# Attention of a hybrid encoder: one maximum over two banks of scores, and turned tiles copied in pairs

## What is computed

```python
s = jnp.einsum('bkgqd,bskd->bkgqs', qi, k, preferred_element_type=F32) * scale
p = jax.nn.softmax(s, axis=-1).astype(v.dtype)
return jnp.einsum('bkgqs,bskd->bkgqd', p, v)
```

## Time and profile before

| what | value |
|---|---|
| median of three runs | 1513.63 us (1511.82 to 1513.84) |
| the profiled execution's own time | 1511.2 us |
| its span in the profile | 1508.5 us |
| mean granted TensorE clock | 0.957 of full |
| attention of the first layer in the span | about 196 to 314 us |
| attention of the second layer in the span | about 933 to 1051 us |

### The profile page before, as it was taken

The page is one execution under the profiler, slowest core; times in us unless marked ns, Lnnn a source line. Parts: engine busy times, 40 slices in busy tenths (PEclk is TensorE's granted clock), DMA queues, the critical chain, the costliest instruction groups (busy, mean ns, idle before and its releaser), DMA issues.

```text
span 1508.5 us, 14989 instructions
## 1 busy us (share of the span) xinstructions
PE 1386.0 (92%) x5763; PEld 1033.6 (69%) x5763; DVE 912.5 (60%) x981; ACT 597.3 (40%) x931; POOL 518.4 (34%) x239
## 2 busy tenths in 40 slices
PE   5999887888999999999979989787979999999997
PEld 4677654455788888878746766454758888887885
DVE  4766776545687777711176776664467887884212
ACT  4422356533534433422242225564344344333222
POOL 2322311015444444344451222100354444444444
PEclk7999998988999999999989999898989999999997
DMA  7211210002233333323241221000213333332331
GB/s 246 83 36 49 49 30 15 1 29 83 70 89 93 98 97 87 92 88 100 82 139 51 61 49 44 15 1 0 71 56 98 91 91 98 98 89 87 99 94 66
DMA packets 203695, 109.93 MB, mean 73 GB/s; under 512 B 14615, under 2 KB 201865, under 8 KB 202730
## 3 DMA queue, kind: packets, MB, share of 16 engines
q1 hardware_dynamic: 203626, 108.98, 24.7%
HBM read 105.69 MB, written 2.10 MB: 71 GB/s over the span
## 4 chain that ended last, share of the span: by engine, by line
PE 78%; DVE 10%; ACT 6%; issue 2%; POOL 2%; DMA 1%; DVEq 0%; POOLq 0%; SPq 0%; ACTq 0%
PE ps L921 20%; PE ps L923 19%; PE ps L922 19%; PE ps L1212 3%; PE ps L1015 2%; PE ps L1028 2%; PE ps L989 2%; PE ps L1188 2%; ACT prob L722 2%; PE ps L1080 1%; DVE p L1427 1%; POOL xT L451 1%; ACT wh L503 1%; PE ps L931 1%; DVE tb L1339 1%
## 5 line engine op out<-in xcount | busy, mean ns | idle before, releaser
L444 POOL TENSOR_TENSOR wl<-raw,wh 128x1024 fp32r<-128x1024 f32 x184 | 447.3, 2432 | 871.7 <-ACT wh L503 871.7
L503 ACT ACTIVATE wh<-raw 128x1024 fp32r<-128x1024 f32 x184 | 195.0, 1060 | 613.3 <-PE ps L923 595.7
L921 PE MATMUL ps<-gh,wh 128*128 128x512 f32 (+1 forms) x896 | 365.7, 408 | 2.7 <-POOL wl L444 2.7
L922 PE MATMUL ps<-gl,wh 128*128 128x512 f32 (+1 forms) x896 | 355.5, 397 | 0.0
L923 PE MATMUL ps<-gh,wl 128*128 128x512 f32 (+1 forms) x896 | 355.3, 397 | 0.0
L921 PEld LDWEIGHTS ps<-gh,wh 128*128 128x128 f32 (+1 forms) x896 | 168.0, 187 | 49.7 <-issue 8.1
L922 PEld LDWEIGHTS ps<-gl,wh 128*128 128x128 f32 (+1 forms) x896 | 167.9, 187 | 45.8 <-issue 5.1
L923 PEld LDWEIGHTS ps<-gh,wl 128*128 128x128 f32 (+1 forms) x896 | 167.8, 187 | 42.1
L1735 DVE SCALAR_TENSOR_TENSOR cv<-pad,pm,cv 128x512 f32<-128x512 f32 x88 | 130.5, 1483 | 84.1 <-ACT cv L823 84.1
L1323 DVE TENSOR_TENSOR acc<-acc,sq 128x512 f32<-128x512 f32 x24 | 60.5, 2520 | 195.8 <-ACT sq L547 195.6
L921 PE MATMUL ps<-fh,wh 128*128 128x512 f32 x352 | 139.5, 396 | 3.2 <-POOL wl L444 3.2
(11 more groups left out here) (231 smaller groups left out, 1902.4 us busy)
## 6 DMA issues: line engine op xcount, KB each, us to landing
raw<-w_up SPq DMA_DIRECT2D x88, 512.0 KB, 3.8
raw<-w_down SPq DMA_DIRECT2D x32, 512.0 KB, 3.6
raw<-w_in SPq DMA_DIRECT2D x30, 512.0 KB, 3.8
raw<-w_out SPq DMA_DIRECT2D x16, 512.0 KB, 3.6
raw<-w_down SPq DMA_DIRECT2D x16, 384.0 KB, 3.1
xio<-x SPq DMA_DIRECT2D x4, 512.0 KB, 4.2
win<-c_win SPq DMA_DIRECT2D x2, 1024.0 KB, 4.9
TF<-c_tf SPq DMA_DIRECT2D x2, 1024.0 KB, 8.8
```

Source lines behind the costliest of these rows:

```text
L444: nc.gpsimd.tensor_tensor(wl[:, slot, :], raw[:, slot, :], wh[:, slot, :].bitcast(F32), ALU.subtract).then_inc(S["lo_ready"], 1)
L503: A(wh[:, slot, :], raw[:, slot, :], ACT.Copy).then_inc(S["hi_ready"], 1)
L921: mm(ps[0:cols, bank, :], w_hi, x_hi, start=start and k == 0, stop=False)
L922: mm(ps[0:cols, bank, :], w_hi, x_lo, start=False, stop=False)
```

## The change

Three things are changed, all inside the attention of both layers.

1. `maxima` takes one instruction for two banks: it reads `ps[:, 0:2, :]` and writes two columns of `nm`, then the same for banks 2 and 3. It waits for both tiles of scores, and the exponentials of both tiles wait for it.
2. ScalarE's `pt_copy(h)` copies banks 4 and 5 in one instruction after the first half of the turning (key tiles 0 and 1). It stands where the copy of tile 0 stood; the copy of tile 2 is gone from ScalarE.
3. VectorE's `pt_copy(h)` copies banks 4 and 5 in one instruction after the second half (key tiles 2 and 3). It stands where the copy of tile 3 stood; the copy of tile 1 is gone from VectorE. So `turn(h, (2, 3))` waits for ScalarE's copy alone, and `turn(h + 1, (0, 1))` and `inverses` wait for VectorE's.

```diff
--- before.py
+++ after.py
@@ -712,7 +712,7 @@
                         A(yh[:, c0 + c, :], src[:, c, :], ACT.Copy).then_inc(S["ygh"], 1)
 
                 def exp(h, qc):
-                    act.wait_ge(S["nmax"], (lay * HEADS + h) * TC + qc + 1)
+                    act.wait_ge(S["nmax"], (lay * HEADS + h) * 2 + qc // 2 + 1)
                     if h >= 2 and qc == 0:
 
                         act.wait_ge(S["pt_tile"], lay * 4 * HEADS + 4 * (h - 1))
@@ -722,13 +722,13 @@
                     A(prob[:, h % 2, qc, :], ps[:, qc, :], ACT.Exp, bias=nm[:, h % 2, qc:qc + 1], scale=1.0,
                       accum_out=den[:, (h // 2) % 2, h % 2, qc:qc + 1]).then_inc(S["p_ready"], 1)
 
-                def pt_copy(h, sc):
-
-                    act.wait_ge(S["pt_tile"], lay * 4 * HEADS + 4 * h + sc + 1)
-                    if h >= 3 and sc == 0:
+                def pt_copy(h):
+
+                    act.wait_ge(S["pt_tile"], lay * 4 * HEADS + 4 * h + 2)
+                    if h >= 3:
 
                         act.wait_ge(S["pv"], lay * PAIRS + (h - 1) // 2)
-                    A(probT[h % 3][:, sc, :], ps[:, 4, :], ACT.Copy).then_inc(S["pt_act"], 1)
+                    A(probT[h % 3][:, 0:2, :], ps[:, 4:6, :], ACT.Copy).then_inc(S["pt_act"], 1)
 
                 def inv_wide(p):
 
@@ -754,13 +754,12 @@
                     if more:
                         exp(h + 1, 0)
                         exp(h + 1, 1)
-                    pt_copy(h, 0)
+                    pt_copy(h)
                     if more:
                         exp(h + 1, 2)
                         exp(h + 1, 3)
                     if h + 2 < GH:
                         q_hi(h + 2)
-                    pt_copy(h, 2)
                     if h and h % 2 == 0:
                         inv_copy(h // 2 - 1)
                     if h % 2:
@@ -1177,10 +1176,12 @@
                     if h == 0:
                         pe.wait_ge(S["evac"], lay * WIN + WIN)
                     for sc in tiles_:
-                        if sc >= 2 or h:
-
-                            k = (lay * HEADS + h) * 2 + sc // 2
-                            pe.wait_ge(S["pt_act" if sc % 2 == 0 else "pt_dve"], k)
+                        if sc % 2 == 0:
+
+                            if sc:
+                                pe.wait_ge(S["pt_act"], lay * HEADS + h + 1)
+                            elif h:
+                                pe.wait_ge(S["pt_dve"], lay * HEADS + h)
                         if sc == 0 and h % 2 and h >= 3:
 
                             pe.wait_ge(S["inv_copy"], lay * PAIRS + h // 2)
@@ -1203,8 +1204,8 @@
                         pe.wait_ge(S["y_pair"], lay * PAIRS + p)
                     if p == GH // 2:
                         pe.wait_ge(S["b7_free"], lay * len(B7) + len(B7))
-                    pe.wait_ge(S["pt_act"], (lay * HEADS + 2 * p + 1) * 2 + 2)
-                    pe.wait_ge(S["pt_dve"], (lay * HEADS + 2 * p + 1) * 2 + 2)
+                    pe.wait_ge(S["pt_act"], lay * HEADS + 2 * p + 2)
+                    pe.wait_ge(S["pt_dve"], lay * HEADS + 2 * p + 2)
                     for sc in range(TC):
                         for half in range(2):
                             h = 2 * p + half
@@ -1223,7 +1224,7 @@
                         bank7(B7_FIRST[h])
                     turn(h, (2, 3))
                     if h and h % 2 == 0:
-                        pe.wait_ge(S["pt_act"], (lay * HEADS + h) * 2 + 2)
+                        pe.wait_ge(S["pt_dve"], lay * HEADS + h + 1)
                         inverses(h // 2 - 1)
                     if h == 0:
                         bank7(B7_FIRST[0])
@@ -1234,7 +1235,7 @@
                     if h == 9:
                         group(1)
                 values(PAIRS - 1)
-                pe.wait_ge(S["pt_act"], (lay * HEADS + HEADS) * 2)
+                pe.wait_ge(S["pt_dve"], lay * HEADS + HEADS)
                 inverses(PAIRS - 1)
 
 
@@ -1498,9 +1499,10 @@
                     tt(dst[:], src[:], hi_[:].bitcast(F32), ALU.subtract).then_inc(S["mlo"], 1)
 
                 def maxima(h):
-                    for qc in range(TC):
-                        dve.wait_ge(S["s_tile"], (lay * HEADS + h) * 4 + qc + 1)
-                        nc.vector.reduce_max(nm[:, h % 2, qc:qc + 1], ps[:, qc, :], AX.X, negate=True).then_inc(S["nmax"], 1)
+                    for qc in range(0, TC, 2):
+                        dve.wait_ge(S["s_tile"], (lay * HEADS + h) * 4 + qc + 2)
+                        nc.vector.reduce_max(nm[:, h % 2, qc:qc + 2], ps[:, qc:qc + 2, :], AX.X, negate=True
+                                             ).then_inc(S["nmax"], 1)
 
                 everything = slice(0, P)
 
@@ -1601,13 +1603,13 @@
                         dve.wait_ge(S["ygh"], lay * DC + c0 + c + 1)
                         tt(yl[:, c0 + c, :], src[:, c, :], yh[:, c0 + c, :].bitcast(F32), ALU.subtract).then_inc(S["ygl"], 1)
 
-                def pt_copy(h, sc):
-
-                    dve.wait_ge(S["pt_tile"], (lay * HEADS + h) * 4 + sc + 1)
-                    if h >= 3 and sc == 1:
+                def pt_copy(h):
+
+                    dve.wait_ge(S["pt_tile"], (lay * HEADS + h) * 4 + 4)
+                    if h >= 3:
 
                         dve.wait_ge(S["pv"], lay * PAIRS + (h - 1) // 2)
-                    copy(probT[h % 3][:, sc, :], ps[:, 5, :]).then_inc(S["pt_dve"], 1)
+                    copy(probT[h % 3][:, 2:4, :], ps[:, 4:6, :]).then_inc(S["pt_dve"], 1)
 
                 def rotate_kr():
 
@@ -1660,12 +1662,11 @@
                 for h in range(HEADS):
                     if h + 1 < HEADS:
                         maxima(h + 1)
-                    pt_copy(h, 1)
                     if h % 2:
                         denominators(h // 2)
                     if h in B7_FIRST and h:
                         bank7(B7_FIRST[h])
-                    pt_copy(h, 3)
+                    pt_copy(h)
                     if h == 0:
                         bank7(B7_FIRST[0])
                     if h and h % 2 == 0:
```

## The result

The changed kernel takes 1532.33 us in the median (1531.0, 1531.43 and 1533.23 us), against 1513.36 us in four executions of the kernel before: ratio 1.013, 95% interval 1.0106 to 1.0154. It is slower by 19 us. A fourth execution of the changed kernel took 2348 us with a granted clock of 0.58 over its whole length, and is not compared.

A forecast was written before the change was run, and what follows sets the result against it. No engine is full; attention is a ring of waits. Lost overlap of 8.3 us per layer, 16.5 for both, plus 2.2 for the clock makes 18.7 on 1513.6: 1532 us, range 1521 to 1543.

The forecast's parts named there:

- faster rival: Attention, 24 heads: VectorE's busy time sets the pace and gains 0.20 us per head, 4.8 us: 1509; chance 0.04.
- (a): Before the exponentials: the first one waits for a maximum of 1.22 us instead of 0.68, +0.54 us.
- (b): In front of the turning's second half: ScalarE's copy takes 1.02 us instead of 0.60, +0.42 us.
- (c): Behind the turning's second half: VectorE's copy waits for both tiles, inverses start after 2.40 us, not 1.35: +1.05 us.
- the gates: Attention places where an engine waits for a piece made longer, by (a), (b) or (c); 16.5 us in both layers.
- The sum over the heads: Attention, heads 0 to 11: costs of waits less head 11's gain, 8.3 us per layer, 16.5 us for both.
- the cover: Head 1: a gap where VectorE idles 1.03 us takes in the later second half; cost 0, without it 0.9.
- Head 11: Last head: second half waits for ScalarE alone, turned during VectorE's four gains, one copy follows: -1.2 us per layer.
- One more stretch per layer: Attention: longer idling drops TensorE to the lower clock once more per layer, at 1.1 us, +2.2 us in both.
- The clock rival: Attention: most lengthened gaps slow TensorE's clock, five more stretches per layer, +11 to +16 us, about 1543; chance 0.16.
- Half the terms hidden: Attention: other waits stand behind the gates, the five (c) terms fall away; costs 8 us, about 1522; chance 0.17.
- No change: Attention: gains at the last head and on VectorE balance the gates, 1514; chance 0.05.

The follow-up runs named there:

- e3: Kernel before, with only ScalarE's copy of the first half of the turning made wide: 1516.4 us, ratio 1.0026.
- e7: Kernel before, with wide maxima and wide first copies of ScalarE only at heads where the forecast has them hidden: 1512.6 us, ratio 1.0003.
- e8: Kernel before, with wide maxima and wide first copies of ScalarE only at heads where the forecast has them waited for: 1520.4 us, ratio 1.005.
- e9: Changed kernel, with unread matmuls laid into TensorE's waits at odd heads: 1515.9 us, ratio 1.0019 to the kernel before.
- e11: Kernel before, with the same unread matmuls in TensorE's waits as e9 and nothing else: 1496.4 us, ratio 0.9892.
- e4: Kernel before, with only VectorE's copy of the second half of the turning made wide: 1516.7 us, ratio 1.0031.
- e6: Changed kernel, with VectorE's four gains moved behind its copy at head 11: 1532.8 us, ratio 1.0146 to the kernel before.

## Why the prediction was right, point by point

**The prices.** Right: 1.218, 1.224 and 1.020 us where 1.22, 1.22 and 1.02 were taken from other wide instructions. The Trainium skill (VectorE: DVE Perf Modes, "The TRN2 errata — SBUF-src ops pay a fixed extra latency per instruction") gives each VectorE instruction from PSUM a fixed part beside what its elements take. Two wide maxima in a row took 2.35 us where four narrow ones took 2.48, so joining saves 0.07 us a pair. The prediction's faster rival was built on such a saving where VectorE sets the pace; e3 takes 7 us of VectorE's work out of each attention and is slower, so here VectorE does not set it.

**(a), (b), (c).** Right in place and size. The first exponential came 1.25 us behind the maxima instead of 0.71, ScalarE's copy holds the second half 1.02 us long, the inverses start 2.41 us behind the second half against 2.40 counted. e7 against e8 shows that (a) and (b) cost only at the gates. (c) costs 1.06 us at head 4 and 1.07 at head 8 in the changed kernel's first layer, where 1.05 was said.

**The sum over the heads.** The starts of TensorE's scores in the first layer, changed less before and less the 0.17 us by which the stage began later, give 0.91 behind head 0 (0.9 said), 1.90 behind head 2 (1.9), 3.13 behind head 3 (2.87), 4.19 behind head 4 (3.92), 5.17 behind head 5 (4.89), 5.29 behind head 6 (5.94), 6.25 behind head 7 (6.91), 7.32 behind head 8 (7.96) and 7.70 behind head 9 (8.41). Heads 4, 5, 7, 8 and 9 added what was said within 0.1 us, head 3 0.26 more. At head 1 TensorE did come 0.93 us later, but the maxima of the next head started only 0.05 later: the cover named there held. Head 2 came out right partly by luck: the sum had ScalarE hold the second half there, but ScalarE's copy ended at 220.76, ahead of it, and TensorE started it at 221.05 straight behind the values, late by what it had lost at head 1. Head 6 added 0.12 us instead of 1.05: its turning ran at the lower clock before (1.84 us) and at the full one now (1.04). In e9 against e11, where this happens less, the first layer's marks end at +9.6; scores of head 7 at the lower clock (3.49 us instead of 1.92) have 1.6 of it, and 8.1 is left, where 8.3 was said. The second layer's end at +12.2, with more of the clock in it, and by the slope both layers come to +8.7. So the code's part is 7.5 us per layer by the changed kernel against the one before and at most 8.7 by e9 against e11, 15.0 to 17.4 in both layers, and the 16.5 that was said lies between.

**Head 11.** Right in kind, too large: between the scores of head 11 and the last values the sum said 1.05 - 1.2, and the marks show +2.0, because the scores of head 11 (5.46 us instead of 4.29) and both halves of the turning (1.69 and 1.94) ran at the lower clock. With the waits filled (e9 against e11, first layer, where part of e9's turning is still slow) head 11 gives back 0.76 us, not 1.2.

**The clock.** The step was right in sign. One more stretch per layer at 1.1 us was taken, 2.2 us in both, and the windows show 27.2 - 20.5 = 6.7 and 35.3 - 27.8 = 7.5 us more at the lower clock, which at 0.35 are 5 us. It is no further stretch, though: the clock up to head 9 is as it was (0.94 in the first layer), and all of it is added at the end of the stage, where TensorE already ran slow (0.73 instead of 0.82). With the code's part at 15.0 us the clock has 5 of the 20 us in the attentions, and then the closeness of 1532 is partly luck, 1.5 us too much in the gates against 3 too little in the clock; with 17.4 it has 2.5, and both terms were right within 1 us. The runs do not decide between them. The clock rival, with five more stretches per layer and 11 to 16 us, was too large either way. Of the rule that waits between bursts throttle TensorE again (Trainium skill, TensorE: Matmul & The Clock Gate, "HAM oscillation — how this bites in real kernels"), e9 and e11 are the test: filled waits, 16 us each.

**The rivals.** Half the terms hidden: falls with the whole 1.06 and 1.07 us at heads 4 and 8 in the changed kernel, and with e4 once the clock is taken out. Faster by VectorE's load: falls with e3. No change: falls with the result.

What stays open: which wait tips the clock at a given place. e4 has longer waits than the kernel before and less time at the lower level, and the traces show only that the stretches move when the waits do. Open too is how the 20 us in the attentions divide more closely than 15.0 to 17.4 us of code and 5 to 2.5 of clock.

## What to carry to other kernels

Two instructions joined into one save the small start of the second, here 0.07 us a pair, and cost the early hand-over of the first half, here 0.4 to 1.05 us, wherever another engine waits for it: count the joined instruction's whole length at each place where its first half releases someone, and join only where nobody waits. Where engines take turns on the same banks, as here in front of the inverses, two engines emptying a bank each beat one engine emptying both by 1.05 us. And before judging a change of a few microseconds in a stage with waits, take the time at the lower clock out of both sides, since it moves from one execution of a kernel to the next (e7's twelve spread over 11 us).

## What the runs showed of the hardware that was not expected

Two layers with the same instructions differ by up to 4 us in 120 with the granted clock (e6, e8), and a microsecond at the lower level costs 0.27 to 0.38 us of time in this stage, in which not every matmul is waited for. Matmuls with no use, laid into waits of 0.3 to 4 us, made the kernel before 1.1% faster (0.9892), and with one reordering on VectorE 1.6% (0.9836), with the granted clock at 1.00 through both attentions.
